# Attention values by head, branch rows split block by block, and waits moved in a three-layer block kernel

## The reference, cut to what matters

```python
h = rms_norm(x, norm_g); proj = h @ w_in
ya = deltanet_branch(...)          # conv, chunked gated delta rule, norm, gate
yb = pooling_branch(...)           # windowed means, 128x128 mix, gate
yc = sparse_attention_branch(...)  # index scores pick 128 keys per query, 4 heads of 128, gate
branches = stack([ya, yb, yc])     # each 512 wide
projected = einsum('btnc,ncd->btnd', branches, w_branch)
gate = sigmoid(gates + gate_b)
x = x + (sum_n gate_n * projected_n) @ w_out
```

## Time and profile before

| | us |
|---|---|
| median of 3 runs (lowest, highest) | 2100.57 (2097.16, 2100.93) |
| the profiled execution | 2101.68 |
| its span | 2099.8 |
| TensorE busy | 2018.2 (96%) |
| VectorE busy | 1076.5 (51%) |
| ScalarE busy | 932.6 (44%) |
| GpSimd busy | 877.6 (42%) |

### The profile page before, as it was taken

How to read it: one execution, slowest core, us unless ns; L and a number is a source line. 1 busy time by engine, 2 the same in 40 slices (tenths; PEclk the granted TensorE clock), 3 DMA queues, 4 the chain that set the end, 5 groups by cost and what they waited for, 6 DMA issues and landing times.

```text
span 2099.8 us, 24567 instructions
## 1 busy us (share of the span) xinstructions
PE 2018.2 (96%) x9468; PEld 1587.5 (76%) x9468; DVE 1076.5 (51%) x1877; ACT 932.6 (44%) x1448; POOL 877.6 (42%) x646
## 2 busy tenths in 40 slices
PE   8999999999999999999999999988999999999999
PEld 6767788777777767787777787666666787888887
DVE  6756854545546657664365646677444256201210
ACT  5565453433345465444333345577445344412421
POOL 5444432334345454431434445456221354444443
PEclk9999999999999999999999999999999999999999
DMA  5234442323434234531423445322111232222232
GB/s 202 75 100 131 136 130 86 136 76 111 153 123 142 90 108 126 151 110 60 162 71 127 169 152 152 124 71 70 61 51 41 79 123 84 99 99 90 101 109 72
DMA packets 90901, 228.47 MB, mean 109 GB/s; under 512 B 25920, under 2 KB 28992, under 8 KB 89472
## 3 DMA queue, kind: packets, MB, share of 16 engines
q1 hardware_dynamic: 89344, 223.74, 32.0%
q10 hardware_dynamic: 1440, 3.15, 0.4%
HBM read 194.99 MB, written 24.64 MB: 105 GB/s over the span
## 4 chain that ended last, share of the span: by engine, by line
PE 70%; DVE 13%; ACT 8%; DMA 2%; issue 2%; POOL 2%; SPq 1%; ACTq 0%; DVEq 0%
PE bank L441 68%; DVE tmp L385 4%; PE bank L444 2%; ACT wh L430 2%; ACT tmp L427 2%; POOL wl L375 1%; SPq L370 1%; DMA pad<-tmp 1%; DVE lt L385 1%; DVE pad L375 1%; ACT pad L430 1%; ACT E L427 1%; ACT L419 1%; DVE nacc L385 1%; ACT lt L427 0%
## 5 line engine op out<-in xcount | busy, mean ns | idle before, releaser
L375 POOL TENSOR_TENSOR wl<-st,wh 128x512 fp32r<-128x512 f32 x606 | 827.7, 1388 | 1174.2 <-ACT wh L430 1174.2
L441 PE MATMUL bank<-hh,wh 128*128 128x512 f32 x1632 | 668.4, 410 | 40.4 <-POOL wl L375 19.8
L441 PE MATMUL bank<-hh,wl 128*128 128x512 f32 x1632 | 640.4, 392 | 0.0
L441 PE MATMUL bank<-hl,wh 128*128 128x512 f32 x1632 | 640.2, 392 | 0.0
L430 ACT ACTIVATE wh<-st 128x1024 fp32r<-128x1024 f32 x303 | 318.2, 1050 | 223.4 <-PE bank L441 183.4
L441 PEld LDWEIGHTS bank<-hh,wh 128*128 128x128 f32 x1632 | 308.9, 189 | 140.6 <-issue 42.0
L441 PEld LDWEIGHTS bank<-hl,wh 128*128 128x128 f32 x1632 | 309.5, 190 | 68.0 <-issue 7.9
L441 PEld LDWEIGHTS bank<-hh,wl 128*128 128x128 f32 x1632 | 308.8, 189 | 67.0
L375 DVE TENSOR_TENSOR xt<-xt,bank 128x512 f32<-128x512 f32 x40 | 27.5, 687 | 243.6 <-PE bank L441 243.6
L385 DVE SCALAR_TENSOR_TENSOR tmp<-pad,col,tmp 128x512 f32<-128x512 f32 x80 | 81.8, 1022 | 41.1 <-ACT tmp L427 39.1
L441 PE MATMUL bank<-fh,wl 128*128 128x512 f32 x256 | 101.1, 395 | 0.0
(11 more groups left out here) (344 smaller groups left out, 3053.9 us busy)
## 6 DMA issues: line engine op xcount, KB each, us to landing
st<-units SPq DMA_DIRECT2D x303, 512.0 KB, 3.5
gates<-tmp SPq DMA_DIRECT2D x48, 256.0 KB, 2.5
gt<-gates SPq DMA_DIRECT2D x48, 256.0 KB, 3.7
pad<-tmp SPq DMA_DIRECT2D x32, 128.0 KB, 3.5
qk<-tmp SPq DMA_DIRECT2D x16, 256.0 KB, 3.1
x_scratch<-xt SPq DMA_DIRECT2D x2, 2048.0 KB, 8.5
xt<-x_scratch SPq DMA_DIRECT2D x2, 2048.0 KB, 8.7
ph<-phi SPq DMA_DIRECT2D x8, 512.0 KB, 5.0
```

The lines of the kernel that those rows point to most:

```text
L375: return NOTHING if self.e is None else self.e.tensor_tensor(out, a, b, op)
L441: return NOTHING if self.e is None else self.e.matmul(out, lhsT, rhs, start=start, stop=stop, skip_group_check=share)
```

## The change

What it does, edit by edit:

- **Attention by head.** The list is `blocks4`, (h, b), head outermost. Px is one tile of 5 x 384, holding for key block i the transposed probabilities of query blocks i to 3 side by side. At steps 6, 10, 14 and 18 (and only there) TensorE makes the values of one head by four matmuls of 512, 384, 256 and 128 columns; it waits there for the copy made at the step before. VectorE multiplies bank 7 into `zc` one head at a time. The gate tile gt0 changes places with the first Px tile.
- **Branch rows per contraction block.** In the last tile of a merge, TensorE signals after each contraction block (`br_k`). ScalarE overwrites yh block by block from there, for branch 0 all four and for branch 2 the first three, and VectorE's splits move with it. Block 3 of branch 2 follows after the attention's end.
- **Banks.** Output-gate tile c uses bank c. `merge3` uses banks 4 to 7.
- **Convolution.** Conv tile 0 uses tmp2 and tmp3, conv tile 1 tmp0 and tmp1, with the waits for their spills.
- **Inverses.** ScalarE's wait for the inverses and its copy come two side steps later, SP's loads of them one side step later.
- **Recurrent branch.** GpSimd's `parts(c - 2)` come ahead of the splits of both units of a round.
- **Others.** SELECT's second number is 14 for 12; RATES[2] 0.501 for 0.511; RATES[4] 0.906 for 0.854. SP's load of the rope tables comes two units after the gate spills, not ahead of them.

```diff
-SELECT = (6, 12, 4)
-RATES = (0.795, 0.764, 0.511, 1.031, 0.854)
+SELECT = (6, 14, 4)
+RATES = (0.795, 0.764, 0.501, 1.031, 0.906)
...
+        L.Px = sb(f"Px{l}", [128, 5 * 384], stack=p3)
...
-    heads4 = [(b, h) for b in range(4) for h in range(4)]
+    blocks4 = [(h, b) for h in range(4) for b in range(4)]
...
+    def conv_tiles(c):
+        return tmp[2 - 2 * (c % 2)], tmp[3 - 2 * (c % 2)]
...
             for c in range(4):
-                yield from tile(("p", l, 4616 + 128 * c), c % 3, ("zc", l, c), g)
+                yield from tile(("p", l, 4616 + 128 * c), c, ("zc", l, c), g)
...
+                        if m == 7 and n != 2 and k < 3:
+                            t.then_inc(*sig("br_k", l, n, k))
...
+                if n >= 6 and n % 4 == 2:
+                    h = u[n - 3][0]
+                    ob = bank(7, "C", l, h)
+                    pe.wait_ge(*at(f"free{4 + (n - 3) % 3}", "sp_p", l, n - 3))
+                    for i in range(4):
+                        pe.wait_ge(*at(f"free{i}", "vs", l, i))
+                        t = pe.mm(ob[:, 128 * i:T], L.vs[:, i, sq4(h)], L.Px[:, 512 * i:384 * i + T], i == 0, i == 3, share=True)
+                    t.then_inc(*sig("sp_o", l, h))
...
-                    o = bank(m % 4, "nu", m)
+                    o = bank(4 + m % 4, "nu", m)
...
                 if c < 2:
-                    ac.wait_ge(*at(f"spill{2 * c}", "gate", l, 3 - 2 * c))
-                    ac.wait_ge(*at(f"spill{2 * c + 1}", "gate", l, 2 - 2 * c))
+                    ac.wait_ge(*at(f"spill{3 - 2 * c}", "gate", l, 2 * c))
+                    ac.wait_ge(*at(f"spill{2 - 2 * c}", "gate", l, 2 * c + 1))
...
-            yield from idle(INVERSE - BACK + 3)
+            yield from idle(INVERSE - BACK + 5)
             ac.wait_ge(*at("inv", l, 31))
...
+                    if n == 1 and (mp, j) == (3, 1):
+                        ac.wait_ge(*at("yAg", l, 3))
+                        for c in range(4):
+                            ac.wait_ge(*read(l, 1, c))
+                            pair(l, 0, c, layer[l].yA[:, c, :])
+                    if n == 0 and (mp, j) == (3, 1):
+                        for c in range(3):
+                            ac.wait_ge(*read(l, 0, c))
+                            ac.wait_ge(*at("free7", "C", l, c))
+                            pair(l, 2, c, layer[l].zc[:, c, :])
...
+                if m == 7 and n != 2:
+                    for c in range(3):
+                        split(l, *((0, c, L.yA[:, c, :]) if n == 1 else (2, c, L.zc[:, c, :])))
...
             for c in range(8):
-                take()
                 if c > 1:
                     parts(c - 2)
-                take()
+                take(2)
...
-            yield from idle(INVERSE - BACK + 4)
+            yield from idle(INVERSE - BACK + 5)
             sp.wait_ge(*at("x_zero", l, False))
```

More of the change, by code:

```diff
@@ L971, in sparse @@
         def sparse(l):
-            L, u = layer[l], heads4
+            L, u = layer[l], blocks4
             yield from idle(8)
             for n in range(len(u) + 4):
[L975 to L983, removed]
+                if n >= 6 and n % 4 == 2:
[6 more added lines that the diff above has]
+                    t.then_inc(*sig("sp_o", l, h))
                 if 2 <= n <= len(u) + 1:
-                    b, h = u[n - 2]
+                    h, b = u[n - 2]
                     o = bank(4 + (n - 2) % 3, "sp_p", l, n - 2)
@@ L991, in sparse @@
                 if n < len(u):
-                    b, h = u[n]
+                    h, b = u[n]
                     nk = 128 * (b + 1)
@@ L1448, in delta @@
             ac.dma(inv_d.rearrange("f n q x c -> (f n q) x c"), L.inv).then_inc(*dma("inverses", l))
-            yield from idle(BACK - 3)
+            yield from idle(BACK - 5)
             def head(h, e):
@@ L1560, in front3, with read @@
             yield from merge(l, 1)
-            ac.wait_ge(*done("br", l, 1, 3))
-            for c in range(4):
-                ac.wait_ge(*at("yAg", l, 3))
-                pair(l, 0, c, L.yA[:, c, :])
             yield from merge(l, 0)
+        def read(l, n, k):
+            return done("br", l, n, 3) if k == 3 else at("br_k", l, n, k)
         def merge(l, n):
@@ L1576, in sparse @@
         def sparse(l):
-            L, u = layer[l], heads4
+            L, u = layer[l], blocks4
+            by_key = L.Px[:].rearrange("p (i s) -> p i s", s=384)
             yield from idle(8)
@@ L1580, in sparse @@
                 if 2 <= n <= len(u) + 1:
-                    b, h = u[n - 2]
+                    h, b = u[n - 2]
                     s = 4 + (n - 2) % 3
+                    to = by_key[:, 0:b + 1, sq4(b)] if b < 3 else by_key[:, 1:5, 0:128]
                     ac.wait_ge(*at("sp_t", l, n - 2))
-                    ac.cp(L.Px[(n - 2) % 3][:, 0:b + 1, :].rearrange("p a b -> p (a b)"), banks[s][:, 0:128 * (b + 1)]).then_inc(*sig(f"free{s}", "sp_p", l, n - 2))
+                    ac.cp(to, banks[s][:, 0:128 * (b + 1)].rearrange("p (a b) -> p a b", b=128)).then_inc(*sig(f"free{s}", "sp_p", l, n - 2))
                 if n < len(u):
-                    b, h = u[n]
+                    h, b = u[n]
                     nk, s = 128 * (b + 1), 2 * (n % 3)
@@ L1850, in scalar_program @@
             ac.wait_ge(*done("br", l, 0, 3))
-            for c in range(4):
-                ac.wait_ge(*at("free7", "C", l, 3))
-                pair(l, 2, c, layer[l].zc[:, c, :])
+            ac.wait_ge(*at("free7", "C", l, 3))
+            pair(l, 2, 3, layer[l].zc[:, 3, :])
             for _ in merge(l, 2):
@@ L2233, in front3, with split @@
             yield from merge(l, 1)
-            for c in range(4):
-                split(0, c, L.yA[:, c, :])
             yield from merge(l, 0)
+        def split(l, n, c, src):
+            L = layer[l]
+            dv.wait_ge(*at("yh", l, n, c))
+            dv.tt(L.yl[:, c, :], src, L.yh[:, c, :].bitcast(F32), ALU.subtract).then_inc(*sig("yl", l, n, c))
         def merge(l, n):
@@ L2250, in merge @@
                     dv.tt(L.acc[:, m, :], L.acc[:, m, :], g[:], ALU.add).then_inc(*sig("acc", l, n, m))
+                if m == 7 and n == 1:
+                    split(l, 0, 3, L.yA[:, 3, :])
                 if n == 2 and m > 0:
@@ L2257, in sparse @@
         def sparse(l):
-            L, u = layer[l], heads4
+            L, u = layer[l], blocks4
             yield from idle(8)
             for n in range(len(u) + 4):
-                if n >= 4 and u[n - 4][1] == 3:
-                    b = u[n - 4][0]
-                    zq = L.zc[:, :, sq4(b)]
-                    dv.wait_ge(*at("sp_o", l, n - 4))
-                    dv.stt(zq, zq, 0.5, f4(banks[7][:]), ALU.mult, ALU.mult).then_inc(*sig("free7", "C", l, b))
+                if n >= 7 and n % 4 == 3:
+                    h = u[n - 4][0]
+                    dv.wait_ge(*at("sp_o", l, h))
+                    dv.stt(L.zc[:, h, :], L.zc[:, h, :], 0.5, banks[7][:], ALU.mult, ALU.mult).then_inc(*sig("free7", "C", l, h))
                 if n < len(u):
-                    b, h = u[n]
+                    h, b = u[n]
                     nk, i = 128 * (b + 1), 2 * (n % 3)
@@ L2542, in vector_program @@
             weave(front3(l), (sparse(l), RATES[2]))
-            for c in range(4):
-                dv.wait_ge(*at("yh", l, 2, c))
-                dv.tt(L.yl[:, c, :], L.zc[:, c, :], L.yh[:, c, :].bitcast(F32), ALU.subtract).then_inc(*sig("yl", l, 2, c))
+            split(l, 2, 3, layer[l].zc[:, 3, :])
             for _ in merge(l, 2):
@@ L2842, in sync_program @@
             sp.dma(L.cdiag[:], cd_d[:, 384:512]).then_inc(*dma("cdiag", l))
-            take(12)
+            take(2)
+            if l == 0:
+                sp.dma(tabs[:, 0:apack.n], tabA).then_inc(*dma("tab", "A"))
+            take(10)
             weave(proj(l), (delta(l), RATES[0]))
```

24 lines of the change are left out of this document (9 added, 15 removed).

## The result

The changed kernel takes **2073.66 us** (median of 4 runs, 2072.44 to 2075.63) against 2100.75 for the kernel before in the same comparison (2097.16 to 2102.25): ratio **0.9874, 95% interval 0.9857 to 0.9892**, that is 27.1 us less. The forecast was 35.7 less (2065), with a range of 2047 to 2083.

A forecast was written before the change was run, and what follows sets the result against it. TensorE, busy 2018 of 2100 us, was taken to bound the kernel. Terms of 2.0, 12.4, 2.0, 3.0, 8.5, 2.4, 1.4 and 6.0 sum to 37.7, less 2 for small waits: 35.7, so 2065, range 2047 to 2083.

The forecast's parts named there:

- the third row: Stretch of the waits for the inverses, 227.9 to 324.0 and 842.7 to 939.2: 12.4 us forecast for both layers.
- selection: Block 2's selection two steps later moves block 3's score products into the recurrence's tail: 2.0 us, bounds -1 and 4.
- the new 0.78: Recurrence's tail: a gap of 0.78 us was forecast to open after the selection's move.
- So both gap and half clock go: 4.5 + 1.7 = 6.2 a layer: TensorE near 255: the 4.5 us gap and its half clock vanish; 12.4 us in all, bounds 5 and 15.
- It fits, barely: Near 250: the following weight unit, landing at 251.3, is split by 255.2; TensorE needs it at 256.3.
- VectorE's own work is unmoved: Stretch of the inverses: moving ScalarE's wait leaves VectorE's work where it was; part of the 12.4 us term.
- Rival 1: The stall changes place: SP behind VectorE's spill delays the next unit; 12.4 becomes about 2, giving 2075; chance 0.13.
- The lock's price: Recurrent branch: one more VectorE convolution operation a round slowed beside GpSimd's splits, 0.8 us.
- the outcome in which the lock eats the gain: Recurrent branch: GpSimd's lock leaves 1 us in place of 6, plus a half-clock stretch: 2072; chance 0.15.
- rivals 4 and 5: Attention: value copy late at every side step, about 2107, chance 0.03; value order costs 8 to 20, about 2080, 0.06.
- The count of half-clock stretches: Whole kernel: at least two fewer stretches of half clock, as a sign that the forecast is right.
- A half clock at new places: Anywhere in the kernel: listed as a sign that the forecast is wrong; no size given.

The follow-up runs named there:

- e1: The changed kernel with ScalarE's wait for the inverses and SyncE's loads of their pieces put back to their old places: 2075.20 us, ratio 0.9895.
- e7: The changed kernel with SyncE's 16 loads of the inverses in four groups a side step apart, the first one step earlier: 2070.45 us, ratio 0.9866.
- e9: The changed kernel with SyncE's spill of a normed row three steps later: 2066.48 us, ratio 0.9845 to the kernel before.
- the five: Five profiles with the changed code from the mark at 225.2 to that at 323.1: mean 96.6 us in layer 0, 95.5 in layer 1.
- e2: The changed kernel with GpSimd's two row parts of the recurrent branch back between the two weight splits: 2078.40 us, ratio 0.9910.
- e3: The changed kernel with the compression's side steps back at 0.854 a main step, from 0.906: 2073.20 us, ratio 0.9887.
- e11: The changed kernel run again, unedited: 2073.18 us, ratio 0.9889 to the kernel before.

## Why the prediction was right, and where it failed

**Right in sign, range and most terms.** 2073.66 lies in 2047 to 2083, but outside the forecast's own 2058 to 2073. With the third row as measured and every other term as forecast it would have been 2078; attention and branch rows, compression and convolution came out 4.7 above their terms together. The compression's share of that, 2.3, is luck (below). Convolution tiles 2.6 (2.0), selection 1.7 (2.0), banks 3.3 (3.0) and branch rows 8.9 (8.5) came as worked out. Block by block the rows leave no wait at all, where 0.1 and 0.4 were left. In the recurrence's tail the first score product took the place of a gap and the second lay in the 1.35; the new 0.78 opened too.

**The step that failed** is the one on ScalarE's wait for the inverses: "So both gap and half clock go: 4.5 + 1.7 = 6.2 a layer". It is about 1 us for both layers in place of 12.4. The working asked whether the next weight unit would be there in time and found room of a microsecond ("It fits, barely"). It followed one queue item, the unit, and left out the two that go the same way. The gate spill behind the same blocked row spill holds ScalarE's gate step until 247.56, so ScalarE comes to the unit, the copy and the row 7.6 us late, as before. "VectorE's own work is unmoved" was wrong too: the high half that ScalarE takes early brings a split of GpSimd beside the inverses, and they end 2 us later. And what TensorE wins at 250 it gives back at the product that waits for lT (283.3 against 283.5 in e1), which hangs on a row swap in SyncE's queue. That this queue, and not VectorE's end, sets the rest of the stretch is shown by e7 and e9, which touch SyncE alone and shorten it by 1.4 to 3.6 us a layer against the means of the five. Rival 1 described this, SyncE behind VectorE's spill, at 2075; it had 0.13 and came within 1.3 us, though the item that is late is a gate spill and not the weight unit. Its argument against ("three units were ready to split when ScalarE returned") was the weak point: they were ready because ScalarE had been held, and in the changed kernel ScalarE takes the first before it is held.

**GpSimd's row parts**: 5.8 by e2 against 6.0 forecast, and rounds of 15.98 against 15.9. Only 4.1 shows against the kernel before, since the compression, now earlier, meets the convolution there: its product waits 4.22. That collision of two edits was not in the sum; e3, without it, has 6.0 in this row. The lock's price was taken as one slow operation more a round; the timeline of VectorE shows it in every other round of this profile (in e3's, in each of the four from 1363.5 on):

```profile
1361.98 4.23 DVE L385 SCALAR_TENSOR_TENSOR lt<-pad,col,lt 128x512 f32<-128x512 f32 x3 [0.84 <-ACT lt L427]
...
1379.39 3.24 DVE L385 SCALAR_TENSOR_TENSOR nacc<-pad,col,nacc 128x512 f32<-128x512 f32 x3 [1.22 <-ACT nacc L427]
```

The first convolution runs while GpSimd does four split instructions in a row from 1360.55 to 1367.33, the second meets one only from 1380.38 on. The Trainium skill ("SBUF — State Buffer", section "SBUF: two separate sides") says that such operations exclude each other for a whole instruction; these rows agree (4.23 against 3.24, 0.99 us for one more operation held), and the outcome in which the lock eats the gain did not come.

**The compression's** load wait went from 1.43 to 0.67 and not to nothing. Most of the 3.7 in the table is half clock: the kernel before has 6.8 us of it behind the wait at 1327, which costs 3.4, and this profile has none there. The same code run again (e11) has it, and needs 131.1 us for the stretch where the kernel before needs 130.7: how much of this row's gain lasts is not shown.

**The attention by head** gave 3.8 by difference (2.4). No wait on the Px copy is among TensorE's waits (the kernel before had 2.0 us), so rivals 4 and 5 had nothing behind them.

**The count of half-clock stretches** was forecast to fall by two. It fell from seven to six. Those behind 562 and 870 are gone, and with them one near 10 us, where the change does nothing. But the one at 255 is now at 254, one stands behind the 2.7 at 283, one of 6.8 us behind the 4.2 at 1367, and the stretches near the end cost 2.9 more, where again the change does nothing. "A half clock at new places" was on the prediction's own list of wrong signs. In all, five stretches of 3.4 us and two of 6.8 became four and two, worth 1.7 us, where the sum had three times 1.7.

## What to carry to other kernels

When a wait is moved behind other work, list everything that waits for the same producer, through every queue in which an item of that producer stands first, and ask for each when it is next needed; one item found in time proves nothing for the others. Ask too what the engine that is set free will start, and whether that slows the producer. When waits only change places, compare whole stretches between two marks and not single waits; here such a stretch followed the order and spacing of an issuing queue (a spill moved three steps down, loads that leave room for others) and not the producer's end. Two edits that each close a gap can meet: check where an advanced side chain now falls on the engine that the other edit made busier.

## What the runs showed of the hardware that was not expected

The length of the wait ahead does not alone decide whether TensorE's clock falls. Windows around the wait before ph,zt, first the changed kernel (2.80 us of wait), then the changed kernel again (e11, 3.29 us); columns as in the earlier trace rows:

```profile
1303.00:1315.00 12.00, 9.20 (x46) 5.75 (x47) 7.66 (x10) 5.93 (x9) 3.73 (x4) 1.00 0.31 98
```

```profile
1306.00:1318.00 12.00, 10.03 (x37) 6.79 (x38) 4.74 (x9) 5.50 (x9) 0.74 (x1) 0.72 0.32 98
```

The same code had the full clock (2.4 GHz) once and a stretch at half of it (1.2 GHz) the other time; its 6.8 us cost 3.4. Here the longer wait had the half clock, but behind the wait before the row's square it is the other way round, 2.98 us in the changed kernel and 3.18 in e11:

```profile
254.60:258.00 3.40, 3.40 (x8) 2.03 (x9) 2.79 (x2) 2.18 (x3) 3.25 (x3) 0.60 0.13 51
```

```profile
254.60:258.00 3.40, 3.40 (x15) 2.56 (x14) 2.75 (x3) 3.08 (x5) 2.85 (x2) 1.00 0.06 23
```

So a profile can differ from the next one of the same kernel by some 3 us a place, and a forecast should give such a stretch a chance, not a certainty.

SyncE's issues in a row are not free: the 16 small loads took its queue from 260.00 to 268.97, 0.56 us each, and what stood behind them in the queue was issued only then.
